# Input projections ahead of the memory rows' products, which move in between the first tile's attention heads

## The chip, the core and the metric

The kernel runs on one core of a Trainium2 chip. The metric is the device time of one execution in microseconds. TensorE (PE) multiplies, VectorE (DVE) and ScalarE (ACT) work on its results, GpSimd (POOL) issues the gathers of expert rows, and SyncE (SP) issues nearly all other transfers. Each engine takes its own instructions in order and waits on semaphores. PSUM holds the products, SBUF everything else.

## The reference, cut to what matters

```python
h   = rmsnorm(x, norm_mix)                      # x: 256 x 1024, float32
qkv_moba, qkv_fox, f = split(h @ w_in)          # w_in: 1024 x 3080, six blocks of 512 columns and 8 gates
o   = [rmsnorm(moba(...)), rmsnorm(fox(...))]   # 8 + 8 heads of 64, causal over 256 rows
x   = x + o @ w_out
mem_n = rmsnorm(mem, norm_mem)                  # mem: 256 x 1024
k, v = mem_n @ w_xk, mem_n @ w_xv               # needed only by the cross-attention
x   = x + softmax((rmsnorm(x) @ w_xq) @ k.T / 16) @ v @ w_xo      # 4 heads of 256
x   = x + peer_ffn(rmsnorm(x))                  # 16 of 16384 experts for each of 8 heads, rows gathered
out = rmsnorm(x, norm_final)
```

The sub-keys of `peer_ffn` (8 x 128 x 64, twice) are transposed once, in the kernel's step `skT`. The products with `w_in`, `w_xk` and `w_xv` don't depend on each other.

## The kernel before

**Tiles and order.** The 256 rows are two tiles of 128. One list, `main`, names the steps in the order in which every engine takes its part of them (lines 128 to 148); an engine skips steps in which it has no part. A step is (name, tile or block, half). There is no scheduler: the written order is the queue of each of PE, ACT and DVE, and SP has an order of its own (lines 390 to 434).

**Half blocks.** A weight block is 1024 x 512 (2 MB), a half block 256 of its columns. Float32 products are made out of three products of rounded parts: high x high, high x low, low x high. So a half block q needs a `split` first: ACT casts the high part into one of two buffers `WH_r[q % 2]` (line 527), DVE subtracts it in place to leave the low part (line 705), and PE then runs 48 matmuls of 128x128 by 128x256 (line 964). `projections(lo, hi)` puts `split` q+2 directly ahead of half block q in `main`. As `split` q+2 overwrites the high part that product q reads, ACT's cast waits until product q has ended, and what comes behind it in ACT's and DVE's queues waits too, the copy of product q out of PSUM first of all.

**The 20 half blocks.** Before: four of `w_xk` (steps `mK`), four of `w_xv` (`mV`), twelve of `w_in` (`winv`, whose result DVE copies, and `wina`, whose result ACT copies, in turn). Then come the 16 heads of tile 0 (8 MoBA, 8 FoX).

**A head.** `S` (PE line 1043, and for FoX 1047 too; DVE adds the mask and takes the minimum, line 750; ACT takes the exponential, line 555), `PT` (PE transposes the probabilities, line 1055; ACT copies, line 560), `O` (PE, line 1064). The heads are staggered: S two ahead, O one behind.

**PSUM banks.** There are two banks for results that DVE takes (`v_bank`: `memT`, `hT`, `winv`, `S`, `skT`, ...) and two for those that ACT takes (`a_bank`: `mK`, `mV`, `wina`, `PT`, ...). Job n of either sort waits until job n-2 of its sort has been copied out (`v_free`, `a_free`). PE is in order, so a transpose that waits for a bank holds up all products behind it.

**SP.** It loads the blocks into six slots in the order of use; a block waits for the last product of the block that had its slot. `bias_scratch` is written to memory and read back in eight pieces while SP waits for it. The sub-keys land in the buffer that held the high part of `h`, so their transfers wait for the last product with `h` (lines 418 to 424). Step `skT` (PE line 1009) stands behind `S` of the first two heads of tile 1.

## Time and profile before

| | us |
|---|---|
| median of three runs (1002.21 to 1005.22) | 1003.92 |
| the profiled execution, its own time | 1000.79 |
| its span in the trace | 999.0 |
| first product of a half block starts | 17.22 |
| last product with `w_in` ends, heads of tile 0 begin | 140.07 |
| last head product of tile 0 starts | 168.88 |
| first probabilities of tile 1 are transposed | 174.84 |
| first gather of expert rows is issued | 312.15 |

Of the whole span PE is busy for 85%, DVE 56%, ACT 42%. Up to 312 us the kernel is a chain of dense steps with hardly any gather; behind it 256 groups of expert rows are fetched at some 400 GB/s and worked off. The change touches only what lies before 174.84 us. The rows of the section below are read as follows: a row gives the start and the duration in us, the engine, the line in the kernel, the operation, `out<-in` with sizes, and in brackets how long the engine had been idle and for whom.

### The profile page before, as it was taken

To read this page: it belongs to the slowest core of one execution; us is meant where nothing else is said; L and a number is where in the kernel's file an instruction comes from. 1 tells how busy PE (TensorE), PEld (TensorE's weight loads), DVE (VectorE), ACT (ScalarE), POOL (GpSimd) and SP (SyncE) were. 2 spreads that over 40 slices of the span, in tenths; PEclk is the share of its full clock that TensorE was granted. 3 is DMA by queue.
4 is the path that set the end of the run, shared out by engine and by line. 5 is a ranking of instruction groups with operands and counts; after the bars stand their busy time and mean duration, and the time that the engine had idled before them with its cause. 6 is when DMAs were issued, how large, how long until landed. Compare 5 with 4: busy or idle time off the path is not lost.

```text
span 999.0 us, 9382 instructions
## 1 busy us (share of the span) xinstructions
PE 847.4 (85%) x3163; PEld 478.0 (48%) x3163; DVE 563.1 (56%) x1336; ACT 416.7 (42%) x1082; POOL 244.0 (24%) x267
## 2 busy tenths in 40 slices
PE   5999999999797988988879999887686877877876
PEld 4999986647745635533334355432232322322322
DVE  5544432112225757477686675758668587685743
ACT  5434434213302454356643543435354344343533
POOL 0000000000002332333333423333333333434330
PEclk9999995585998999999999999999999999999999
DMA  9869652000016998999999999999999999999995
GB/s 335 289 144 382 225 212 63 22 0 1 1 41 266 367 406 311 372 423 423 420 415 403 364 423 366 360 423 378 420 421 422 421 420 422 409 407 418 416 422 237
DMA packets 63299, 316.33 MB, mean 317 GB/s; under 512 B 7891, under 2 KB 10004, under 8 KB 30484
## 3 DMA queue, kind: packets, MB, share of 16 engines
q0 software_dynamic: 36864, 268.45, 65.9%
q1 hardware_dynamic: 26340, 47.28, 14.1%
q8 instruction: 25, 0.41, 0.2%
q14 instruction: 22, 0.18, 0.0%
q10 hardware_dynamic: 48, 0.01, 0.0%
HBM read 313.10 MB, written 2.62 MB: 316 GB/s over the span
## 4 chain that ended last, share of the span: by engine, by line
PE 48%; DMA 27%; DVE 15%; ACT 7%; issue 2%; POOL 0%; POOLq 0%; DVEq 0%; ACTq 0%
DMA qkvb<-in_expert_rows,expert_idx 20%; PE y L1152 10%; PE a_bank L964 8%; DMA spare<-in_expert_rows,expert_idx 7%; PE v_bank L1152 7%; PE a_bank L957 6%; PE v_bank L957 6%; DVE qkvb L890 5%; PE v_bank L964 4%; PE v_bank L1043 2%; PE y L1064 2%; DVE spare L890 2%; PE v_bank L1047 1%; ACT diag L617 1%; DVE key_idx L828 1%
## 5 line engine op out<-in xcount | busy, mean ns | idle before, releaser
L462 POOL DMA_INDIRECT qkvb<-in_expert_rows,expert_idx x172 | 162.1, 943 | 592.3 <-DVE expert_idx L866 309.7
L1152 PE MATMUL v_bank<-qkvb,diag 128*128 128x512 f32 x344 | 169.4, 627 | 48.7 <-ACT diag L617 48.7
L610 ACT ACTIVATE gelu<-dots 128x1 f32<-128x1 f32 x256 | 51.6, 202 | 347.6 <-DVE dots L890 347.2
L1152 PE MATMUL y<-qkvb,diag 128*128 128x512 f32 x344 | 166.1, 626 | 35.8 <-ACT diag L617 35.7
L890 DVE CUSTOM_DVE_ANT_0 qkvb<-h_psum,qkvb 128x1024 f32<-128x1024 f32 x86 | 104.2, 1223 | 75.0 <-DMA qkvb<-in_expert_rows,expert_idx 74.8
L890 DVE CUSTOM_DVE_ANT_0 qkvb<-a_bank,qkvb 128x1024 f32<-128x1024 f32 x86 | 104.2, 1223 | 69.6 <-DMA qkvb<-in_expert_rows,expert_idx 68.9
L1152 PEld LDWEIGHTS v_bank<-qkvb,diag 128*128 128x128 f32 x344 | 61.8, 193 | 155.7 <-ACT diag L617 103.2
L1152 PEld LDWEIGHTS y<-qkvb,diag 128*128 128x128 f32 x344 | 64.7, 197 | 126.3 <-issue 63.1
L462 POOL DMA_INDIRECT spare<-in_expert_rows,expert_idx x84 | 80.3, 956 | 142.0 <-PE y L1152 74.2
L617 ACT ACTIVATE diag<-ident,wgt 128x128 f32<-128x128 f32 x256 | 102.7, 401 | 8.3
L1152 PE MATMUL v_bank<-spare,diag 128*128 128x512 f32 x168 | 84.2, 634 | 22.3 <-ACT diag L617 22.3
L1152 PE MATMUL y<-spare,diag 128*128 128x512 f32 x168 | 77.9, 602 | 12.2 <-ACT diag L617 12.2
L614 ACT ACTIVATE wgt<-gelu,gates 128x1 f32<-128x1 f32 x256 | 75.4, 295 | 8.3
L705 DVE TENSOR_TENSOR weights_r<-weights,spare_r 128x2048 fp32r<-128x2048 f32 x20 | 45.7, 2291 | 54.3 <-ACT spare_r L527 54.3
L890 DVE CUSTOM_DVE_ANT_0 spare<-h_psum,spare 128x1024 f32<-128x1024 f32 x42 | 50.8, 1223 | 39.7 <-DMA spare<-in_expert_rows,expert_idx 39.6
L890 DVE CUSTOM_DVE_ANT_0 spare<-a_bank,spare 128x1024 f32<-128x1024 f32 x42 | 50.9, 1223 | 34.6 <-DMA spare<-in_expert_rows,expert_idx 34.4
L1152 PEld LDWEIGHTS v_bank<-spare,diag 128*128 128x128 f32 x168 | 30.5, 196 | 75.2 <-ACT diag L617 49.0
L527 ACT CAST spare_r<-weights 128x2048 fp32r<-128x2048 f32 x20 | 37.9, 1901 | 59.6 <-PE a_bank L964 43.1
L1152 PEld LDWEIGHTS y<-spare,diag 128*128 128x128 f32 x168 | 30.6, 191 | 52.8 <-issue 29.5
L957 PEld LDWEIGHTS a_bank<-x_and_h,weights 128*128 128x128 f32 x448 | 53.7, 201 | 3.6 <-issue 3.6
L957 PE MATMUL a_bank<-x_and_h,weights 128*128 128x128 f32 x448 | 53.9, 284 | 0.8 <-issue 0.8
L555 ACT ACTIVATE probs<-s_sb,neg_max 128x128 f32<-128x128 f32 (+1 forms) x32 | 14.5, 454 | 56.1 <-DVE neg_max L750 56.1
(194 smaller groups left out, 1163.1 us busy)
## 6 DMA issues: line engine op xcount, KB each, us to landing
weights<-in_w_in SPq DMA_DIRECT2D x6, 2048.0 KB, 18.5
weights<-in_w_xk SPq DMA_DIRECT2D x2, 2048.0 KB, 12.7
weights<-in_w_xv SPq DMA_DIRECT2D x2, 2048.0 KB, 15.5
weights<-in_w_out SPq DMA_DIRECT2D x2, 2048.0 KB, 18.3
weights<-in_w_xq SPq DMA_DIRECT2D x2, 2048.0 KB, 8.0
weights<-in_w_xo SPq DMA_DIRECT2D x2, 2048.0 KB, 8.2
weights<-in_w_peer_query SPq DMA_DIRECT2D x2, 2048.0 KB, 7.9
qkvb<-in_expert_rows,expert_idx POOLq DMA_INDIRECT x172
```

Source lines behind the costliest of these rows:

```text
L462: pool.indirect_dma_start(ROWS[n % NS], None, expert_rows, bass.IndirectOffsetOnAxis(ap=IDX[:, H % 3, k:k + 1], axis=0))\
L527: act.copy(WH_r[t % 2], half_block(t, W)).then_inc(high_ready, 1)
L610: nc.scalar.activation(gel[:, i:i + 1], dots[:, i:i + 1], ACT.Gelu).then_inc(gelu_done, 1)
L614: nc.scalar.activation(wgt[:, i:i + 1], gel[:, i:i + 1], ACT.Copy, scale=GATE[:, H % 3, k:k + 1])\
L617: nc.scalar.activation(diag[:, i, :], ident[:, :], ACT.Copy, scale=wgt[:, i:i + 1])\
L705: nc.vector.tensor_tensor(half_block(t, W_r), half_block(t, W), WH_r[t % 2].bitcast(f32), ALU.subtract).then_inc(low_ready, 1)
L890: nc.vector.tensor_tensor_reduce(out=ROWS[i][:, 0:D], in0=HP[n // SPT][:, :], in1=ROWS[i][:, 0:D], scale=1.0, scalar=0.0, op0=ALU.mult, op ...
L957: ins = nc.tensor.matmul(bank[:, lo:lo + n], lhs(k), rhs(k), start=(k == 0), stop=(k == chunks - 1))
L964: ins = nc.tensor.matmul(bank[:, lo:lo + n], a(k), b(k), start=(k == 0 and p == 0), stop=(k == KC - 1 and p == 2))
L1043: ins = nc.tensor.matmul(bank[:, 0:nk], Q[lo:lo + HD, t, c, :], K[lo:lo + HD, 0:t + 1, c, :], start=True, stop=i < NH)
L1064: ins = nc.tensor.matmul(y[:, i * HD:(i + 1) * HD], PT[:, n % 2, j * P:(j + 1) * P], V[:, j, i * HD:(i + 1) * HD], start=(j == 0), stop=(j ...
L1152: ins = nc.tensor.matmul(YP[t][:, b * BLK:(b + 1) * BLK], diag[:, i, :], ROWS[i][:, D + b * BLK:D + (b + 1) * BLK], start=False, stop=n % ...
```

## The change

The blocks' order becomes `w_in`, `w_xk`, `w_xv`. The rows of x are loaded, normed and transposed (`hT`) first. The memory rows are loaded behind the second block of `w_in`, and their steps (`root_m`, `scale_m`, `memT`, `m_parts`) stand between the third, fourth and fifth half products. The eight half products with the memory rows stand between tile 0's heads, one behind every second head. The memory rows' parts move out of Q, K into a slot of the weight buffer (slot 5), which later takes the second block of `w_xq`; so that block, and all that stands behind it in SP's queue (the first block of `w_peer_query`, the sub-keys, `w_xo`), waits for the last `mV` product.

```diff
@@ the block list and the slots @@
+MEM_SLOT = 5
...
-    for name, cols in (("w_xk", 2), ("w_xv", 2), ("w_in", 6), ("w_out", 2), ("w_xq", 2), ("w_xo", 2),
+    for name, cols in (("w_in", 6), ("w_xk", 2), ("w_xv", 2), ("w_out", 2), ("w_xq", 2), ("w_xo", 2),
                        ("w_peer_query", 2)):
         blocks += [(name, b) for b in range(cols)]
-    BN = {key: n for n, key in enumerate(blocks)}
+
+    SLOT = dict(zip(blocks, (0, 1, 2, 3, 4, 0, 1, 2, 3, 4, 0, 1, 2, MEM_SLOT, 3, 4, 0, 1)))
+    NTH = {key: [k for k in blocks if SLOT[k] == SLOT[key]].index(key) + 1 for key in blocks}
+    BEFORE = {key: [k for k in blocks if SLOT[k] == SLOT[key]][NTH[key] - 2] for key in blocks if NTH[key] > 1}
...
@@ the order of the steps @@
-    main = [("root_m", 0, 0), ("scale_m", 0, 0), ("root_m", 0, 1), ("scale_m", 0, 1), ("gains", 0, 0),
-            ("memT", 0, 0), ("memT", 0, 1), ("memT", 1, 0), ("memT", 1, 1), ("m_parts", 0, 0),
-            ("m_parts", 1, 0), ("split", 0, 0), ("split", 1, 0), ("bias", 0, 0), ("root_h", 0, 0), ("root_h", 1, 0),
-            ("scale_h", 0, 0), ("scale_h", 1, 0), half_job(0)]
-    main += [("hT", t, i) for t in range(T) for i in range(2)] + [("split", 2, 0)] + projections(1, 2)
-    main += projections(2, 3) + [("h_parts", 0, 0), ("h_parts", 1, 0), ("f_parts", 0, 0)]
-    main += projections(3, 8) + [("forget", 0, 0)]
-    main += projections(8, 10) + [("fsum", 0, 0)] + projections(10, len(halves))
-    main += heads(0, 0, 2 * NH) + [("o_out", 0, 0), ("o_out", 0, 1), ("o_root", 0, 0), ("o_root", 0, 1)]
+    def mem_tile(m):
+        return [("root_m", 0, m), ("scale_m", 0, m)], [("memT", m, 0), ("memT", m, 1), ("m_parts", m, 0)]
+
+    main = [("root_h", 0, 0), ("scale_h", 0, 0), ("root_h", 1, 0), ("scale_h", 1, 0), ("gains", 0, 0)]
+    main += [("hT", 0, 0), ("hT", 0, 1), ("split", 0, 0), ("h_parts", 0, 0), ("hT", 1, 0), ("hT", 1, 1),
+             ("h_parts", 1, 0), ("split", 1, 0), ("bias", 0, 0), ("f_parts", 0, 0)]
+    main += projections(0, 2) + mem_tile(0)[0] + projections(2, 3) + mem_tile(0)[1]
+    main += projections(3, 4) + mem_tile(1)[0] + projections(4, 5) + mem_tile(1)[1]
+    main += projections(5, 7) + [("forget", 0, 0)] + projections(7, 9) + [("fsum", 0, 0)] + projections(9, 12)
+    first = heads(0, 0, 2 * NH)
+    for h in range(2 * NH):
+        at = first.index(("O", 0, h))
+        main += first[:at]
+        first = first[at:]
+        if h % 2:
+            main += projections(12 + h // 2, 13 + h // 2)
+    main += first + [("o_out", 0, 0), ("o_out", 0, 1), ("o_root", 0, 0), ("o_root", 0, 1)]
...
@@ where the memory rows' copies lie @@
-        MH_r = QKVB_r[:, 0:2, :]
-        M_whole, ML_r = QKVB[:, 2:4, :], QKVB_r[:, 2:4, :]
+        MEMS, MEMS_r = [of[:, MEM_SLOT, :].rearrange("p (h m x) -> p h m x", h=2, m=2) for of in (W, W_r)]
+        MH_r = MEMS_r[:, 0, :, :]
+        M_whole, ML_r = MEMS[:, 1, :, :], MEMS_r[:, 1, :, :]
...
-        MEM = [Q[:, m, :, :].rearrange("p c x -> p (c x)") for m in range(2)]
-        MEMT = [K[:, m, :, :] for m in range(2)]
+        MEM = [MEMS[:, 0, m, :] for m in range(2)]
+        MEMT = [MEMS[:, 1, m, :].rearrange("p (c x) -> p c x", c=KC) for m in range(2)]
...
@@ SyncE: new queue @@
+            def load_block(name, b):
+                key = (name, b)
+                if key in BEFORE:
+                    sp.wait_ge(*used_up(*BEFORE[key]))
                 src = A[name][0].rearrange("(k p) c -> p k c", p=P)[:, :, b * BLK:(b + 1) * BLK]
+                sp.dma_start(W[:, SLOT[key], :].rearrange("p (k c) -> p k c", k=KC), src)\
+                    .then_inc(w_full[SLOT[key]], 16)
+
+            for t in range(T):
+                sp.dma_start(X[t], A["x"][0, t * P:(t + 1) * P, :]).then_inc(ld_x[t], 16)
             load_gain(sp, 1)
             load_gain(sp, 2)
+            load_block("w_in", 0)
             sp.wait_ge(rel_one, 1)
             sp.dma_start(relb[0:N_BUCKETS, :], A["rel_bias"]).then_inc(ld_rel, 16)
             sp.dma_start(onehot, A["bucket_rows"]).then_inc(ld_rel, 16)
             sp.dma_start(bf[:, :], A["b_forget"][0].rearrange("(h a) -> h a", a=1)).then_inc(ld_wf, 16)
             sp.dma_start(wf[:, :, :], A["w_in"][0].rearrange("(k p) c -> p k c", p=P)[:, :, 6 * BLK:6 * BLK + NH])\
                 .then_inc(ld_wf, 16)
+            load_block("w_in", 1)
+            for m in range(2):
+                sp.dma_start(MEM[m], A["mem"][0, m * P:(m + 1) * P, :]).then_inc(ld_mem[m], 16)
+            for b in range(2, 5):
+                load_block("w_in", b)
 
 
             sp.wait_ge(a_free, AN[("bias", 0, 0)] + 1)
             sp.dma_start(bias_scratch, brow.unsqueeze(1).broadcast_to([NH, P, FDIST])).then_inc(brow_out, 16)
             sp.wait_ge(brow_out, 16)
             for h in range(NH):
                 toeplitz = bass.AP(tensor=bias_scratch.tensor, offset=h * P * FDIST + P - 1,
                                    ap=[[FDIST - 1, P], [1, SEQ]])
                 sp.dma_start(B[:, h, :], toeplitz).then_inc(ld_bias, 16)
+            load_block("w_in", 5)
+            for name in ("w_xk", "w_xv", "w_out"):
+                for b in range(2):
+                    load_block(name, b)
+            load_block("w_xq", 0)
+
+
+            sp.wait_ge(a_full, AN[("mV", 1, 1)] + 1)
+            load_block("w_xq", 1)
+            sp.dma_start(wq_early, A["w_peer_query"][0].rearrange("(k p) c -> p k c", p=P)[:, :, 0:BLK])\
+                .then_inc(ld_early, 16)
+            for half, name in enumerate(("peer_subkeys_1", "peer_subkeys_2")):
+                sp.dma_start(sk_nat[:, :, half * HD:(half + 1) * HD], A[name][0].rearrange("h n d -> n h d"))\
+                    .then_inc(ld_sk, 16)
+            for b in range(2):
+                load_block("w_xo", b)
+            sp.wait_ge(v_full, VN[("skT", 0, 1)] + 1)
+            sp.dma_start(gffn[:, :], A["norm_ffn"][0:1, :].broadcast_to([P, D])).then_inc(ld_gffn, 16)
+            for b in range(2):
+                load_block("w_peer_query", b)
...
@@ ScalarE: the memory rows' square goes to hp, and root_h waits for nothing else @@
-                    root(key, MEM[i], V[:, i, :], D)
+                    root(key, MEM[i], hp[:, :], D)
                 elif name == "root_h":
                     act.wait_ge(ld_x[t], 16)
-                    act.wait_ge(sq_done, 2)
```

DVE's queue at the memory rows (`L662`/`L680` apply the gain to a transposed half of them, `L692`/`L710` take the low part, `L705`/`L723` is the subtraction of a split, `L736`/`L754` copies a `winv` product out of its bank). Before, at the start of the kernel:

```order
L678 COPY gain_cols<-v_bank 128x32
L662 TENSOR_TENSOR qkvb<-v_bank,gain_cols 128x512 x4
L692 TENSOR_TENSOR qkvb_r<-qkvb,qkvb_r 128x1024 x2
L705 TENSOR_TENSOR weights_r<-weights,spare_r 128x8x256 x2
L655 RECIPROCAL stat<-stat 128x1
L685 TENSOR_SCALAR qkvb<-x_and_h,stat 128x1024
```

Now, between the half products:

```order
L700 TENSOR_SCALAR weights<-weights,stat 128x1024
L723 TENSOR_TENSOR weights_r<-weights,spare_r 128x8x256
L754 TENSOR_SCALAR qkvb<-v_bank 128x2x2x128
L680 TENSOR_TENSOR weights<-v_bank,gain_cols 128x512 x2
L710 TENSOR_TENSOR weights_r<-weights,weights_r 128x1024
L723 TENSOR_TENSOR weights_r<-weights,spare_r 128x8x256
```

The gains of the memory rows moved from the kernel's start to behind a split and the copy of a product; PE has the eight transposes of a memory tile in one piece (`L969`) ahead of the fourth product, and again ahead of the sixth.

ACT's queue at the first heads (`L555`/`L573` is a head's exponential, `L560`/`L578` copies its transposed probabilities, `L527`/`L545` is the cast of a split, `L506`/`L525` copies a product with `w_xk`). Before:

```order
L555 ACT_TABLE_LOAD
L555 ACTIVATE probs,row_sum<-s_sb,neg_max 128x128 x2
L560 COPY probs_t<-a_bank 128x128
L555 ACTIVATE probs,row_sum<-s_sb,neg_max 128x128
L560 COPY probs_t<-a_bank 128x128
L555 ACTIVATE probs,row_sum<-s_sb,neg_max 128x128
L560 COPY probs_t<-a_bank 128x128
L555 ACTIVATE probs,row_sum<-s_sb,neg_max 128x128
L560 COPY probs_t<-a_bank 128x128
L555 ACTIVATE probs,row_sum<-s_sb,neg_max 128x128
L560 COPY probs_t<-a_bank 128x128
```

Now:

```order
L578 COPY probs_t<-a_bank 128x128
L573 ACTIVATE probs,row_sum<-s_sb,neg_max 128x128
L578 COPY probs_t<-a_bank 128x128
L573 ACTIVATE probs,row_sum<-s_sb,neg_max 128x128
L545 CAST spare_r<-weights 128x2048
L525 COPY mem_k<-a_bank 128x512
L578 COPY probs_t<-a_bank 128x128
L573 ACTIVATE probs,row_sum<-s_sb,neg_max 128x128
L578 COPY probs_t<-a_bank 128x128
L573 ACTIVATE probs,row_sum<-s_sb,neg_max 128x128
L545 CAST spare_r<-weights 128x2048
L525 COPY mem_k<-a_bank 128x512
```

A cast and the copy of a product came in behind every second head. The cast stands ahead of the product's copy and of the next head's copy and exponential.

SP's queue around the sub-keys. Before:

```order
L387 DMA weights<-in_w_in 128x8x512 x3
L387 DMA weights<-in_w_out 128x8x512 x2
L387 DMA weights<-in_w_xq 128x8x512 x2
L387 DMA weights<-in_w_xo 128x8x512 x2
L420 DMA spare<-in_w_peer_query 128x8x512
L423 DMA scaled_gffn<-in_peer_subkeys 128x8x64 x2
L426 DMA scaled_gffn<-in_norm_ffn 128x1024
```

Now:

```order
L400 DMA weights<-in_w_xv 128x8x512 x2
L400 DMA weights<-in_w_out 128x8x512 x2
L400 DMA weights<-in_w_xq 128x8x512 x2
L437 DMA spare<-in_w_peer_query 128x8x512
L440 DMA scaled_gffn<-in_peer_subkeys 128x8x64 x2
L400 DMA weights<-in_w_xo 128x8x512 x2
L445 DMA scaled_gffn<-in_norm_ffn 128x1024
```

The sub-keys stood behind both blocks of `w_xo` and behind the wait for the last product with `h`, which ended ahead of all heads; now they stand behind the second block of `w_xq`, and so behind the wait for the last `mV` product, which comes ahead of the last head's `O`. `w_xo` follows them.

## Rows read from the trace of the kernel before

**Rows 1.** the chain of waits, 0 to 420 us: start us, us, what (merged)

```profile
17.22 8.14 PE a_bank L964 x48
...
27.89 40.31 PE a_bank L964 x336
...
174.84 0.69 PE a_bank L1055 x2
```

**Rows 2.** by stretch: PE, PEld, DVE, ACT, POOL busy, PEclk, DMA share, GB/s

```profile
76.70:140.00 63.30, 63.30 (x528) 63.15 (x527) 27.92 (x19) 24.87 (x19) 0.00 (x0) 1.00 0.73 264
140.00:168.00 28.00, 26.01 (x89) 18.30 (x89) 4.68 (x32) 12.55 (x46) 0.00 (x0) 0.59 0.52 169
```

**Rows 3.** timeline of ACT, 60 to 100 us

```profile
68.30 1.91 ACT L527 CAST spare_r<-weights 128x2048 fp32r<-128x2048 f32 x1 [3.37 <-PE a_bank L964]
70.11 0.58 ACT L510 COPY mem_v<-a_bank 128x512 f32<-128x512 f32 x1
```

**Rows 4.** timeline of DVE, 60 to 100 us

```profile
78.72 2.29 DVE L705 TENSOR_TENSOR weights_r<-weights,spare_r 128x2048 fp32r<-128x2048 f32 x1 [5.04 <-ACT spare_r L527]
80.93 0.68 DVE L736 TENSOR_SCALAR qkvb<-v_bank 128x512 f32<-128x512 f32 x1
```

**Rows 5.** timeline of all engines, 0 to 28 us

```profile
7.98 0.69 DVE L662 TENSOR_TENSOR qkvb<-v_bank,gain_cols 128x512 f32<-128x512 f32 x1
...
11.78 2.42 DVE L692 TENSOR_TENSOR qkvb_r<-qkvb,qkvb_r 128x1024 fp32r<-128x1024 f32 x2
11.90 1.04 ACT L514 CAST qkvb_r<-qkvb 128x1024 fp32r<-128x1024 f32 x1 [0.92 <-DVE qkvb L662]
12.85 3.69 ACT L527 CAST spare_r<-weights 128x2048 fp32r<-128x2048 f32 x2
```

**Rows 6.** the weight tile's transfers issued 0 to 5 us: the first block

```profile
DMA to landing us min/median/max: 9.9/9.9/9.9
```

**Rows 7.** timeline of all engines, 138 to 178 us

```profile
140.09 0.58 ACT L542 COPY qkvb<-a_bank 128x512 f32<-128x512 f32 x1 [9.06 <-PE a_bank L964]
...
141.25 0.29 DVE L750 CUSTOM_DVE_ANT_0 s_sb<-v_bank,qkvb 128x128 f32<-128x128 f32 x1 [6.23 <-PE v_bank L1043]
...
143.21 0.33 PE L1055 MATMUL a_bank<-ident,probs 128*128 128x128 f32 x1
...
143.47 0.48 PE L1043 MATMUL v_bank<-qkvb 64*128 64x128 f32 x2
...
143.88 0.43 PE L1064 MATMUL y<-qkvb,probs_t 128*128 128x64 f32 x2
...
144.45 0.29 PEld L1043 LDWEIGHTS v_bank<-qkvb 64*128 64x128 f32 x2
...
168.88 1.25 PE L1064 MATMUL y<-qkvb,probs_t 128*128 128x64 f32 x4
...
171.90 1.94 PE L952 MATMUL v_bank<-ident,scaled_gffn 128*128 128x128 f32 x8 [0.61 <-DVE neg_max L750]
```

**Rows 8.** by stretch, as rows 2: the clock falls, PE busy and PE idle

```profile
144.00:145.00 1.00, 1.00 (x6) 0.74 (x7) 0.31 (x3) 0.94 (x6) 0.00 (x0) 1.00 1.05 410
145.00:146.00 1.00, 1.00 (x5) 0.78 (x5) 0.28 (x2) 0.66 (x3) 0.00 (x0) 0.50 1.04 401
...
318.00:320.00 2.00, 0.00 (x0) 0.00 (x0) 0.13 (x1) 0.56 (x1) 1.15 (x2) 0.77 1.03 430
```

**Rows 9.** SyncE's DMA issues, 0 to 310 us

```profile
69.66 3.67 SPq L415 DMA_DIRECT2D qkvb<-bias_scratch  x8
...
140.57 0.51 SPq L420 DMA_DIRECT2D spare<-in_w_peer_query  x1
141.12 9.13 SPq L423 DMA_DIRECT2D scaled_gffn<-in_peer_subkeys  x2
```

**Rows 10.** the two sub-key transfers, issued 141.12 and 144.5 us

```profile
DMA to landing us min/median/max: 11.4/12.7/14.0
```

**Rows 11.** by stretch, as rows 2: behind the sub-keys' landing

```profile
155.00:160.00 5.00, 5.00 (x16) 3.51 (x16) 0.60 (x4) 1.70 (x7) 0.00 (x0) 0.50 0.01 2
```

More of the change, by code:

```diff
@@ L280, in wslot @@
         def wslot(name, b):
-            return BN[(name, b)] % W_SLOTS
+            return SLOT[(name, b)]
         def wblk(name, b):
@@ L399, in _ @@
             sp.dma_start(onehot, A["bucket_rows"]).then_inc(ld_rel, 16)
-            load_block(1)
             sp.dma_start(bf[:, :], A["b_forget"][0].rearrange("(h a) -> h a", a=1)).then_inc(ld_wf, 16)
@@ L403, in _ @@
                 .then_inc(ld_wf, 16)
-            for n in range(2, W_SLOTS):
-                load_block(n)
+            load_block("w_in", 1)
[3 more added lines that the diff above has]
+                load_block("w_in", b)
             sp.wait_ge(a_free, AN[("bias", 0, 0)] + 1)
             sp.dma_start(bias_scratch, brow.unsqueeze(1).broadcast_to([NH, P, FDIST])).then_inc(brow_out, 16)
-            load_block(W_SLOTS)
             sp.wait_ge(brow_out, 16)
@@ L415, in _ @@
                 sp.dma_start(B[:, h, :], toeplitz).then_inc(ld_bias, 16)
-            for n in range(W_SLOTS + 1, len(blocks)):
-                if n == BN[("w_peer_query", 0)]:
-                    sp.wait_ge(a_full, AN[("wina", 5, 1)] + 1)
-                    sp.wait_ge(v_full, VN[("winv", 5, 0)] + 1)
-                    sp.dma_start(wq_early, A["w_peer_query"][0].rearrange("(k p) c -> p k c", p=P)[:, :, 0:BLK])\
-                        .then_inc(ld_early, 16)
-                    for half, name in enumerate(("peer_subkeys_1", "peer_subkeys_2")):
-                        sp.dma_start(sk_nat[:, :, half * HD:(half + 1) * HD], A[name][0].rearrange("h n d -> n h d"))\
-                            .then_inc(ld_sk, 16)
-                    sp.wait_ge(v_full, VN[("skT", 0, 1)] + 1)
-                    sp.dma_start(gffn[:, :], A["norm_ffn"][0:1, :].broadcast_to([P, D])).then_inc(ld_gffn, 16)
-                load_block(n)
+            load_block("w_in", 5)
[16 more added lines that the diff above has]
+                load_block("w_peer_query", b)
             sp.wait_ge(v_full, VN[("xo", 1, 0)] + 1)
@@ L520, in step @@
                     wname, b, half = halves[t]
-                    n = BN[(wname, b)]
-                    act.wait_ge(w_full[n % W_SLOTS], 16 * (n // W_SLOTS + 1))
+                    act.wait_ge(w_full[SLOT[(wname, b)]], 16 * NTH[(wname, b)])
                     if t >= 2:
@@ L942, in weights @@
             def weights(name, b):
-                n = BN[(name, b)]
-                pe.wait_ge(w_full[n % W_SLOTS], 16 * (n // W_SLOTS + 1))
+                pe.wait_ge(w_full[SLOT[(name, b)]], 16 * NTH[(name, b)])
                 return wblk(name, b)
```

11 lines of the change are left out of this document (removed).

## Prediction

> **What bounds the kernel now.** I read the chain of waits first, then the busy time by stretch, then the timelines of ACT and DVE beside a half product, last SyncE's issues and their landings. The chain shows where the change acts: the first half product runs from 17.22 for 8.14 us, and the next seven take 40.31 us without a gap, 5.76 us each (336 matmuls, 48 to a product) [rows 1]. From 76.70 to 140.00 PE is busy for 63.30 of 63.30 us at the full clock (granted share 1.00, 2.4 GHz); in the 28 us of tile 0's heads behind it PE is busy for 26.01 us, but at a mean share of 0.59 [rows 2]. So the reader is to see two stages, both bound by PE: a dense one, and one whose work is small and runs at 1.2 GHz. The heads take from 140.07 (ACT's copy of the last product starts at 140.09) to the last `O` at 168.88, 28.8 us; tile 1 goes on at 174.84 [rows 1, 7]. The idea worth testing is that the 46 us of memory products would cover the heads' waits and hold the clock up. What decides is whether PE can go from a head to a product and back without waiting for ACT and DVE.
>
> Beside a product these are not idle. Behind each product's end ACT casts (68.30 to 70.21) and only then copies the product out (70.11 for 0.58) [rows 3]: the bank is free 2.5 us after the product's end (which is 68.21, from rows 1: 27.89 + 40.31). DVE subtracts for 2.29 us and copies at 80.93 for 0.68 [rows 4]; that cast began at 76.79 by the same pattern, so a bank on DVE's side is free 4.9 us after the product's end. Before, all this lies under the next product of 5.76 us, since PE always has one with the other sort of bank.
>
> **The change part by part.** The number of half products (20), splits (20) and head steps is the same. I sum what comes ahead of 174.84.
>
> *Start.* Before, the first weight block landed at 2.37 + 9.9 = 12.3 us [rows 6], and x shared the DMA engines with it. Now x comes first and the block has the engines nearly to itself: some 1.3 us earlier by half a megabyte less at 410 GB/s [rows 8], so 11.0. Then in DVE's and ACT's order: cast 1.85, subtraction 2.29, low part of h 1.21 (half of 2.42), two gains of 0.69, and only behind those ACT's cast of the second tile's h 1.04 and its low part 1.21 [rows 5]. That is 9.0 us, a first product at 20.2 in place of 17.22: +3.0. If the block lands no earlier, +4.3; if the casts hid each other wholly as before, 0. I take 3.0. It starts at half clock as before, 8.14 us.
>
> *hT moved ahead.* The gap between the first and the second product, 25.36 (17.22 + 8.14) to 27.89, held the transposes of h [rows 1]. It goes: -2.5.
>
> *memT.* PE has eight transposes ahead of the fourth product and eight ahead of the sixth. The second four need the bank of the `winv` product that has just ended, and DVE copies that behind the split: 4.9 us, then four transposes of some 0.5 us (1.94 for eight at half clock [rows 7]). PE stands and the next product is behind: 5.5 us, twice, +11.0. Bounds: if DVE copied at once, little more than the transposes, 2.5 for both; at the high end nothing but the clock. The other additions on ACT (square 1.04, cast 1.04) and DVE (scale, low part 1.21) fit into the 5.76 us beside 2.5 and 3.0 us of split and copy, so 0; should ACT write the square to PSUM at twice the price it still fits.
>
> *The heads.* Three sorts of gap. (1) From the last `w_in` product to the first memory product: before, DVE took S of head 0 at 141.25; now the split's subtraction stands ahead of it and it starts at +4.3 (1.9 + 2.3, with a hand-over). From there to the end of head 4's S took 141.25 to 144.45 and 0.4 for the S [rows 7], 3.6 us: 7.9. (2) Behind six of the products a cast stands ahead of the product's copy on ACT. PE does O, PT, S, O in less than 1 us, then its PT wants the bank of that product: 2.5 us, then PT and S, 0.67 us (143.21 to 143.88 [rows 7]), with FoX's second matmul some 0.35 more. 3.2 once, 3.55 four times, 2.85 for the one without S. (3) Behind the seventh there is no cast: 0.8. Sum 7.9 + 3.2 + 14.2 + 2.85 + 0.8 = 28.95, against 28.8 before: 0. The heads no longer cost PE time at half clock; they cost waits of the same length. If the gaps were only the heads' own matmuls at full clock (S, O and PT from 143.47 to 144.45 [rows 7], 0.98 a head, with FoX's second matmul 1.33), 18.5 us: -10.3.
>
> *The clock.* It fell at 145, five us behind the last product, though PE was full of head work again, and elsewhere in the middle of 318 to 320, where PE was idle [rows 8]. The two memT gaps (5.5 us) and the 7.9 us one are like these. A product that begins at half clock cost 8.14 - 5.76 = 2.4 more [rows 1]: three times, +7.2, between 0 and 7.2. The seven short gaps: between 0 and 7 x 2.4 = 16.8; I take 0, since each holds only 1.8 us with PE idle, and keep 16.8 for the range.
>
> The Trainium skill ("TensorE: Matmul & The Clock Gate", HAM oscillation) describes the bad case: matmul bursts with waits between, each burst started cold. Rows 8 agree for long gaps; whether 3.3 us is one, no row shows. By the rule applied to every product the time is the first rival's.
>
> *Sub-keys.* Before, they were issued right behind the 140.07 end together with 4 MB of blocks, and the second landed at 144.5 + 11.4 = 155.9 (the first at 155.1) [rows 9, 10]; behind it the engines moved 2 GB/s [rows 11]. That lay under the heads, `skT` ran at 171.90. Now the same burst (w_xq's second block, w_peer_query's first, sub-keys) waits for the last mV product, behind which PE has one O, two S and then `skT`. Landing 15.8 us behind it, eight transposes 1.94, a hand-over: tile 1 goes on 17.9 us after the start of the last O, where it was 174.84 - 168.88 = 6.0. +11.9. Nothing covers it: DVE and ACT wait behind `skT` too. Bounds: 4.7 MB at the 430 GB/s of rows 8 are 10.9 us, so +7; with both transfers fully late (14.0 behind 144.5) +14.5.
> The Trainium skill ("DMA: Bandwidth & Descriptors", Queues, rings and completion order) says a ring's descriptors are consumed in order, so sub-keys can't overtake the blocks; by its 425 GB/s the estimate would be 11 us in place of 15.8.
>
> *Hidden.* The last w_in block now follows the write and read-back of the bias. If that read-back is issued at 69.66 as before [rows 9] and the block lands 10 to 19 us behind it, it is there by 92 at the latest; its split is due at about 93. 0, with a few us above. `w_xo` is loaded 20 us later but used far behind. The stages from 174.84 on keep their length, at half clock first as before, and the gathers start later by the sum.
>
> **Sum.** +3.0 - 2.5 + 11.0 + 0 + 7.2 + 11.9 = +30.6. The profiled execution took 1000.79 us, so 1031.4; it lies 3.1 below the median 1003.92, which gives 1034.5 for a median.
>
> **Rivals.**
> (A) Every product starts cold: the short gaps count as idle for the clock too. For: the heads kept it down with PE full. Against: between gaps stand 5.76 us of dense work. 1034.5 + 16.8 = 1051.
> (B) The sub-keys don't hold tile 1 up, or much less, and the clock stays up in the long gaps: 1034.5 - 11.9 = 1022.5; by the clock alone 1027. For: bytes alone need less than 15.8. Against: rows 10 and 11.
> (C) Not slower: the splits don't stand in the way. One mechanism, at every bank behind a product: the casts would run ahead, under the product before, so that the bank is free at the product's end. Then memT costs 2.5 in place of 11.0, the heads -10.3, the start's +3.0 goes and the clock holds (-7.2): 1034.5 - 29.0 = 1005.5, inside 0.3%; with the sub-keys by bytes alone (-4.9) 1000.6. It decides from the point where a product's copy follows it within 1 us. Against it: rows 3, where the cast comes first, and the written order keeps it so.
> (D) It doesn't do what it says, e.g. the last w_in block late: some 5 to 10 us more, in the range.
>
> **How the numbers follow.** Forecast 0.72, with its own range 1024 to 1045; (A) 0.12; (B) 0.10; (C) 0.06, a third of it faster. Range 1021 to 1048: it leaves out (C) and most of (A). A measurement of this kernel tells 0.3%, 3 us, from no change. Faster 0.02, within 0.04, slower 0.94.
>
> **What would show it.** First product at 20 to 21.5 us; PE idle over 4 us ahead of the second four memT transposes, twice; last w_in product ending near 110; six gaps of 3.2 to 3.6 us between memory products, in which PT waits for ACT's copy; the last mV product ending near 187; `skT` waiting for DMA to near 203, PT of tile 1 near 205. Wrong would be: a first product before 18, memory products back to back, `skT` without a wait, or a stage behind 205 that is shorter than before's.

## The result and the profile after

| | before | after |
|---|---|---|
| median of the runs, us | 1003.07 (4 runs) | 1051.66 (1047.82 to 1055.28, 4 runs) |
| ratio, 95% interval | | 1.0483 (1.0439 to 1.0527) |
| the profiled execution, its own time | 1000.79 | 1051.51 |
| its span | 999.0 | 1049.7 |
| first half product starts, us from the span's start | 17.22 | 21.30 |
| last `w_in` product ends | 140.07 | 112.08 |
| last memory product ends | 68.21 | 204.69 |
| tile 1 goes on (first transposed probabilities) | 174.84 | 222.31 |
| first gather of expert rows | 312.15 | 358.79 |

The changed kernel is 4.8% slower: 48.6 us by the medians, 50.7 by the two profiled executions. 47.5 us of it stand at 222.31, where tile 1 goes on; up to the first gather nothing is added (46.6), and behind it 4.1 (690.9 against 686.8 us), of which more below. One execution of all that are told of below, of the kernel of experiment 9, took 1083.7 us at a mean granted clock of 0.73, where its others had 0.93 to 0.94; it is left out.

The page's second part of the changed kernel shows PE's busy tenths and its granted clock in 40 slices of 26 us:

```profile
PE   3889789769989798898788989987778878778786
...
PEclk7889877858599999899999999999999999999999
```

Before had six nines and then two slices at 5 (the heads, from 150 us on). Now the second to the eighth slice read 8, 8, 9, 8, 7, 7, 8. The first slice says nothing on the change: the trace of before shows a share of 1.00 there, although its first product took 8.14 us with 0.41 us for a matmul in place of 0.28. There the duration tells the clock, not the share. The chain of waits of the changed kernel (start us, us, what), which answers to rows 1:

```profile
21.30 8.64 PE v_bank L981 x48
...
43.48 2.29 DVE weights_r L723
45.77 0.61 DVE qkvb L754
...
46.52 1.09 PE v_bank L969 x4
47.61 7.36 PE a_bank L981 x48
...
66.88 7.90 PE a_bank L981 x48
...
112.16 1.91 ACT spare_r L545
...
114.15 2.15 issue
...
121.05 8.28 PE a_bank L981 x48
...
132.65 7.45 PE a_bank L981 x48
...
144.14 8.62 PE a_bank L981 x48
...
198.66 6.03 PE a_bank L981 x48
...
208.99 11.30 DMA scaled_gffn<-in_peer_subkeys
...
222.31 0.43 PE a_bank L1072 x2
```

Each step stands where the prediction put it. The first product starts at 21.30. Ahead of the fourth product DVE subtracts, copies the third, PE transposes, and the product (47.61) takes 7.36 us. Behind the last `w_in` product (112.08) come ACT's cast and DVE's subtraction (the row of 2.15, for which the profile names no releaser), and the first memory product starts at 121.05. Then the products themselves: 8.28, 7.45, 8.62 and so on, 6.03 for the last. Seven of the eight are far from the 5.76 of [rows 1]; the prediction had that for the first alone.

The timeline of one gap between two memory products in the changed kernel (start us, us, engine, instruction; what lies between one product's end and the next one's start I call a gap, whether PE is busy in it or not), which answers to rows 3 and 7:

```profile
129.40 1.90 ACT L545 CAST spare_r<-weights 128x2048 fp32r<-128x2048 f32 x1 [7.49 <-PE a_bank L981]
...
129.94 0.43 PE L1081 MATMUL y<-qkvb,probs_t 128*128 128x64 f32 x2
131.21 0.58 ACT L525 COPY mem_k<-a_bank 128x512 f32<-128x512 f32 x1
...
131.93 0.30 PE L1072 MATMUL a_bank<-ident,probs 128*128 128x128 f32 x1 [1.56 <-ACT mem_k L525]
...
132.58 0.51 PE L981 MATMUL a_bank<-weights_r,spare_r 128*128 128x256 f32 x2
```

The product's last matmul ended at 129.3. PE did O, PT, S and O up to 130.4, then stood for 1.56 us until ACT's copy of the product, behind the cast, had freed the bank; PT at 131.93, next product at 132.58. This is the predicted gap of 3.2 us, to a tenth (3.25 by this timeline, 3.32 by the chain). What the clock made of it, by stretch (columns as rows 2, the third number from the end is the granted share):

```profile
44.00:45.00 1.00, 0.00 (x0) 0.00 (x0) 1.00 (x1) 0.00 (x0) 0.00 (x0) 0.67 0.45 49
...
132.00:133.00 1.00, 1.00 (x6) 0.76 (x7) 1.00 (x1) 0.00 (x0) 0.00 (x0) 1.00 0.00 0
133.00:134.00 1.00, 1.00 (x7) 1.00 (x6) 1.00 (x5) 0.13 (x1) 0.00 (x0) 0.55 0.09 16
```

In the wait for the memory rows' bank the share falls at 44.3, 2.9 us behind the product's end, with PE idle all that time. In the heads it falls at 133.1, though PE had stood for only 1.56 us and was in the next product already. SyncE's issues of the changed kernel, answering to rows 9:

```profile
163.94 41.13 SPq L400 DMA_DIRECT2D weights<-in_w_xq  x2
205.12 0.58 SPq L437 DMA_DIRECT2D spare<-in_w_peer_query  x1
205.75 8.45 SPq L440 DMA_DIRECT2D scaled_gffn<-in_peer_subkeys  x2
```

The block of `w_xq` waited to 204.7, and the sub-keys are behind it; the landing in the chain (208.99 + 11.30 = 220.3) is 15.6 us behind the last product's end, against 15.8 in [rows 9, 10]. The blocks issued ahead of them landed ahead of them, `w_xq`'s at 212.4 and `w_peer_query`'s at 218.0.

### The profile page after: what moved, and what is told of

Read it like the earlier page. It is cut to its first block, busy times and chain, and to the rows that moved or that the text cites. A ratio compares the mean times of both kernels' runs of the same rounds, so it can differ in the third digit from the quotient of the medians.

```text
span 1049.7 us, 9379 instructions
## 1 busy us (share of the span) xinstructions
PE 860.5 (82%) x3163; PEld 490.4 (47%) x3163; DVE 562.1 (54%) x1336; ACT 415.2 (40%) x1082; POOL 243.3 (23%) x267
## 4 chain that ended last, share of the span: by engine, by line
PE 45%; DMA 29%; DVE 14%; ACT 7%; issue 3%; SPq 1%; POOL 0%; POOLq 0%; ACTq 0%; DVEq 0%
DMA qkvb<-in_expert_rows,expert_idx 19%; PE a_bank L981 9%; PE y L1169 9%; DMA spare<-in_expert_rows,expert_idx 9%; PE v_bank L1169 6%; PE a_bank L974 6%; PE v_bank L974 5%; DVE qkvb L908 4%; PE v_bank L981 4%; DVE spare L908 2%; PE v_bank L1060 2%; PE y L1081 1%; ACT diag L635 1%; DVE key_idx L846 1%; DMA scaled_gffn<-in_peer_subkeys 1%
## 5 line engine op out<-in xcount | busy, mean ns | idle before, releaser
L1169 PE MATMUL v_bank<-qkvb,diag 128*128 128x512 f32 x344 | 173.0, 638 | 47.3 <-ACT diag L635 47.3
L723 DVE TENSOR_TENSOR weights_r<-weights,spare_r 128x2048 fp32r<-128x2048 f32 x20 | 45.8, 2292 | 107.4 <-ACT spare_r L545 107.4
L1169 PE MATMUL v_bank<-spare,diag 128*128 128x512 f32 x168 | 82.3, 621 | 22.4 <-ACT diag L635 22.4
L545 ACT CAST spare_r<-weights 128x2048 fp32r<-128x2048 f32 x20 | 38.0, 1900 | 92.0 <-PE a_bank L981 64.8
L974 PEld LDWEIGHTS a_bank<-x_and_h,weights 128*128 128x128 f32 x448 | 53.3, 199 | 3.7 <-issue 3.7
L981 PE MATMUL a_bank<-weights_r 128*128 128x256 f32 x128 | 42.4, 331 | 0.0
```

The source lines that it names most:

```text
L545: act.copy(WH_r[t % 2], half_block(t, W)).then_inc(high_ready, 1)
L723: nc.vector.tensor_tensor(half_block(t, W_r), half_block(t, W), WH_r[t % 2].bitcast(f32), ALU.subtract).then_inc(low_ready, 1)
L974: ins = nc.tensor.matmul(bank[:, lo:lo + n], lhs(k), rhs(k), start=(k == 0), stop=(k == chunks - 1))
L981: ins = nc.tensor.matmul(bank[:, lo:lo + n], a(k), b(k), start=(k == 0 and p == 0), stop=(k == KC - 1 and p == 2))
L1169: ins = nc.tensor.matmul(YP[t][:, b * BLK:(b + 1) * BLK], diag[:, i, :], ROWS[i][:, D + b * BLK:D + (b + 1) * BLK], start=False, stop=n % ...
```

## The experiments

All ratios are against the kernel before, run on the same chip as the kernels of its group; its medians in these groups were 1001.9 to 1002.6 us. "The changed kernel" is 1051.7, from the group of the result, where before had 1003.1: a difference from it in us is good to a us or two, and where it matters the point at which tile 1 goes on (222.31 in the changed kernel) is given from the traces.

**1. Memory products in one piece, ahead of the heads.**

```diff
+    main += projections(12, len(halves))
     first = heads(0, 0, 2 * NH)
...
-        if h % 2:
-            main += projections(12 + h // 2, 13 + h // 2)
```

> Edit: the changed kernel, but the eight memory products stand in one piece behind the input products and ahead of tile 0's heads (no interleaving); block order, start, memory rows' steps and SyncE's queue stay as changed. Theory (the interleaving costs): the stretch from the last input product's end to the last head's O took 92.6 us in the changed kernel, where 8 x 5.76 + 28.8 = 74.9 would do without interleaving; and the sub-keys, issued behind the last memory product, again land under the heads (-11.6): 1051.7 - 17.7 - 11.6 = 1022. Rival (the loss is in the start and the memory rows' transposes, or behind the heads, and interleaving is neutral): no more than the 11.6 us of the sub-keys, 1040. The clock in the memory products should be 1.00 throughout and each 5.76 us.

1020.1 us (before in this group 1001.9), ratio 1.0186 (1.0152 to 1.0220). From 111 to 158 us, by stretch:

```profile
111.00:158.00 47.00, 46.71 (x390) 46.38 (x388) 16.31 (x10) 17.96 (x17) 0.00 (x0) 1.00 0.39 135
```

Clock 1.00, PE busy for 46.71 of 47 us. Interleaving, with the late sub-keys that it brings, cost 31.5 us. The rest of the loss, 18 us, lies in what this kernel shares with the changed one, the start and the memory rows' transposes. The rival is out.

**2. The gaps filled with dense work.**

```diff
                 elif name == "PT":
                     n = SN[(t, i)]
+                    if t == 0 and i in (4, 6, 8, 10, 12, 14):
+                        for k in range(14):
+                            nc.tensor.matmul(hp[:, 0:HC], h_high(k % KC)[:, 0, :], h_high(k % KC),
+                                             start=True, stop=True)
                     pe.wait_ge(p_ready, n + 1)
```

> Edit: the changed kernel with 14 more dense matmuls (128x128 by 128x256, of the normed rows with themselves, into an unused bank, results not read) put into six of the gaps between memory products, right ahead of the PT that waits for ACT's copy. PE has more to do and nothing waits less. Theory (it is the clock: gaps of 3.2 to 4.0 us let it fall, and the products behind them run at 1.2 GHz for a part): seven products behind such gaps took 7.45, 8.62, 7.43, 8.66, 7.44, 7.32 and 6.03 us; six of them go to 5.76 with a granted clock of 1.00, 12 us less: 1040, although PE executes 84 matmuls (10 us) more. Rival (the products are slow since ACT and DVE work beside them, or since the gap itself costs): no gain, 1052, or up to 10 us slower if the added matmuls don't fit into the wait.

1038.8 us, ratio 1.0372 (1.0333 to 1.0411): 12.9 us less than the changed kernel, with more to do. The chain of this run at the first gap:

```profile
129.24 0.37 PE y L1085 x2
129.60 1.71 PE h_psum L1071 x14
131.32 0.15 PE a_bank L1076
131.47 0.41 PE v_bank L1060 x2
131.88 5.95 PE a_bank L981 x48
```

The 14 matmuls (1.71 us) fill what was a wait, the gap is still 3.3 us long, and the product behind it takes 5.95 us, not 7.45; so do the next five (5.94 or 5.95, the sixth 5.77). By stretch, the whole of the heads in this run and in the changed kernel:

```profile
111.00:194.00 83.00, 78.17 (x571) 72.42 (x569) 20.85 (x42) 29.02 (x65) 0.00 (x0) 0.94 0.22 77
...
112.20:204.70 92.50, 80.12 (x480) 73.97 (x480) 20.61 (x41) 28.55 (x64) 0.00 (x0) 0.80 0.20 69
```

From 126 us on, behind the first product, the share of this run is 1.00 up to 194; what is missing to 1.00 in its row lies ahead of that. The gaps behind products got no shorter (all seven together 23.5 us in place of 22.4), and the neighbours on ACT and DVE are the same; only PE's own activity in the gaps differs. The six products fell from 46.9 to 35.5 us, by 11.4. So it is the clock, and not the waits or a contention, that lengthened the products. This is the run that settles the missed term.

**3. Splits one product later between the heads.**

```diff
-    main += projections(5, 7) + [("forget", 0, 0)] + projections(7, 9) + [("fsum", 0, 0)] + projections(9, 12)
+    main += projections(5, 7) + [("forget", 0, 0)] + projections(7, 9) + [("fsum", 0, 0)] + projections(9, 11) + [half_job(11)]
...
-            main += projections(12 + h // 2, 13 + h // 2)
+            q = 12 + h // 2
+            main += ([("split", q + 1, 0)] if q + 1 < len(halves) else []) + [half_job(q)]
```

> Edit: the changed kernel, but between the heads split q+1 stands ahead of product q (its buffer has been free since product q-1 ended), in place of split q+2, which had to wait for product q itself; the split ahead of the last input product goes too. The same work, interleaved in the same places. Theory (gaps come from the cast standing ahead of the product's copy on ACT, and the clock falls in them): the copy follows the product's end at once, gaps shrink from 3.2 to 4.0 us to 1.3 to 2 us, products go to 5.76 us but the first (some 8), head 0 starts 3 us earlier: the stretch goes from 92.6 to about 65 us, 1051.7 - 28 = 1024. Rival (the heads' own chain from S over DVE and ACT to PT and O sets the gaps): gaps stay over 3 us, 1045 to 1052.

1022.7 us, ratio 1.0211 (1.0168 to 1.0254), 29 us less than the changed kernel. Its chain:

```profile
116.43 8.34 PE a_bank L982 x48
124.78 0.17 PE y L1082 x2
...
125.84 0.12 PE a_bank L1073
...
126.37 5.95 PE a_bank L982 x48
```

The gap is 1.6 us (124.78 to 126.37), all of it matmuls, and the products take 5.95. From the last `w_in` product's end (111.07) to the last memory product's (179.44) it is 68.4 us, in place of 92.6. Of these 24.2 us, 3.6 are the first wait, shorter since the split ahead of the last input product is gone, and 20.6 the gaps and products behind it. Only the first product (8.34) still starts cold, behind a wait of 5.4 us for the first exponentials. This is the same interleaving, place for place, without the cast in ACT's way: the gaps came from the queue's order, and the heads' chain doesn't set them.

**4. Sub-keys issued early.** In SyncE's queue the two transfers go behind the first `w_out` block, with a wait for the last products with `h`.

```diff
-            for name in ("w_xk", "w_xv", "w_out"):
-                for b in range(2):
-                    load_block(name, b)
+            for name, b in (("w_xk", 0), ("w_xk", 1), ("w_xv", 0), ("w_xv", 1), ("w_out", 0)):
+                load_block(name, b)
+            sp.wait_ge(v_full, VN[("winv", 5, 0)] + 1)
+            for half, name in enumerate(("peer_subkeys_1", "peer_subkeys_2")):
+                sp.dma_start(sk_nat[:, :, half * HD:(half + 1) * HD], A[name][0].rearrange("h n d -> n h d"))\
+                    .then_inc(ld_sk, 16)
+            load_block("w_out", 1)
...
-            for half, name in enumerate(("peer_subkeys_1", "peer_subkeys_2")):
-                sp.dma_start(sk_nat[:, :, half * HD:(half + 1) * HD], A[name][0].rearrange("h n d -> n h d"))\
-                    .then_inc(ld_sk, 16)
```

> Edit: the changed kernel, but the two sub-key transfers are issued behind the first block of w_out (right after the last input product), in place of behind the second block of w_xq and the wait for the last memory product. Theory (tile 1 waited 11.6 us for the sub-keys alone): the wait of skT goes and tile 1's first transposed probabilities follow the last O by about 6 us, not 17.6: 1051.7 - 11.6 = 1040. Rival (something else is as late, the table load and the exponentials, or the freed transfers collide with others): less than half of that, over 1046.

1034.5 us, ratio 1.0329 (1.0280 to 1.0378), 17 us less; expected were 11.6. The chain of this run behind the last product (202.16):

```profile
203.41 1.28 ACT L503
...
205.96 1.28 ACT L574
...
207.90 0.44 PE a_bank L1073 x2
```

Now the two table loads and the exponentials of ACT end last, as before the change, and tile 1 goes on 5.7 us behind the last product (17.6 in the changed kernel): 11.9 us, the predicted term. The last product itself ended 2.5 us earlier than in the changed kernel with nothing changed on PE, ACT or DVE. The trace has most of it at the start: the first block landed 9.2 us behind its issue in place of 10.0, the first product started at 20.55 in place of 21.30 and took 7.78 in place of 8.64 us, and the products behind the two waits for the memory rows took 0.6 us less together. Such a shift is no effect of the edit. The rest of the 17 is in the difference of two medians with some us between their runs.

**5. Copy and memory transposes ahead of the split.**

```diff
-    main += projections(0, 2) + mem_tile(0)[0] + projections(2, 3) + mem_tile(0)[1]
-    main += projections(3, 4) + mem_tile(1)[0] + projections(4, 5) + mem_tile(1)[1]
+    def swapped(q, m):
+        return mem_tile(m)[0] + [half_job(q)] + mem_tile(m)[1][:2] + [("split", q + 2, 0)] + mem_tile(m)[1][2:]
+    main += projections(0, 2) + swapped(2, 0) + projections(3, 4) + swapped(4, 1)
```

> Edit: the changed kernel, but the third and the fifth input product's copy and the memory rows' transposes stand ahead of the next split in the list, no longer behind it. Theory (PE stood for 6.1 us twice, since DVE's copy of the product stood behind the split's subtraction, and the clock fell in it): PE's two gaps go from 6.1 to about 1.5 us each (copy 0.7, transposes 0.5), the products behind them from 7.36 and 7.90 to 5.76: -9.2 - 3.7 = -13, 1039. Rival (the split comes later now and the product after next waits for its low part): -9 + a wait of 1 to 4 us twice, 1043 to 1050.

1036.9 us, ratio 1.0330 (1.0290 to 1.0369), 14.8 us less. The chain at the first tile of memory rows:

```profile
35.32 5.78 PE v_bank L983 x48
...
41.12 0.70 DVE qkvb L756
41.82 0.14 issue
41.96 0.63 PE v_bank L971 x4
42.59 5.75 PE a_bank L983 x48
```

The gap is 1.5 us (41.10 to 42.59) in place of 6.1, and the product behind it takes 5.75 in place of 7.36. The later split costs nothing.

**6. The start's order.** The four `hT` steps and both `h_parts` ahead of `split` 0.

```diff
-    main += [("hT", 0, 0), ("hT", 0, 1), ("split", 0, 0), ("h_parts", 0, 0), ("hT", 1, 0), ("hT", 1, 1),
-             ("h_parts", 1, 0), ("split", 1, 0), ("bias", 0, 0), ("f_parts", 0, 0)]
+    main += [("hT", 0, 0), ("hT", 0, 1), ("hT", 1, 0), ("hT", 1, 1), ("h_parts", 0, 0),
+             ("h_parts", 1, 0), ("split", 0, 0), ("split", 1, 0), ("bias", 0, 0), ("f_parts", 0, 0)]
```

> Edit: the changed kernel, but the transposes of both x tiles and both casts of h stand ahead of the first split. Theory (the first product started 4.1 us later since the second tile's gains and low part stood behind the first split): it starts at 17.3 in place of 21.3: -4, 1047.7. Rival (the first weight block's landing at 12.3 us sets it and all else is beside it): no change, 1051.

1046.5 us, ratio 1.0424 (1.0378 to 1.0471), 5.2 us less; the first product starts at 17.22 in its chain, to the hundredth as before. The block landed at 11.9 here (12.3 in the kernel before and in the changed one), and the chain no longer passes through it, but through the rows of x, their transposes and casts, and then the split. In the changed kernel 9.0 us of work stood between the landing and the first product.

**7. All four mended.**

> Edit: the changed kernel with all four mended: splits one product later between the heads, sub-keys issued behind the first w_out block, copies and memory transposes ahead of the split, and all four hT transposes and both casts of h ahead of the first split (first product at 17.3 as before, -4). Theory (the terms are of one chain and add up): 1051.7 - 29 - 17 - 13 - 4 = 989 in place of about 1003 of before: faster by 1.4%. Rival (they overlap: what one gives back another takes, as each wait hides the next): 1000 to 1010, no better than before.

996.6 us (8 runs), ratio 0.9929 (0.9899 to 0.9959): faster than before, but by 0.7% in place of 1.4%. Tile 1 goes on at 169.04, 5.8 us ahead of before and 53.3 ahead of the changed kernel. The four single runs, each read at that same point, had given 5.2, 13.9, 14.4 and 25.2, together 58.7. A small new wait is in the chain:

```profile
68.57 10.21 DMA weights<-in_w_in
...
78.80 1.91 ACT spare_r L549
...
83.17 5.99 PE v_bank L985 x48
```

The last `w_in` block, behind the write and the read-back of the bias, now is due before it lands: the late block that the prediction had under (D), here worth 1 us (PE stands for 1.00 us ahead of this product, which starts at 83.17; in the kernel of 8, where the same block came sooner, it starts at 82.28). Of the 5.4 us between 58.7 and 53.3 that is 1.0. Another 3.5 were no effects of the edits: the shift of 2.5 in experiment 4, and 1.0 in experiment 3, whose last `w_in` product also ended earlier (111.07 in place of 112.08) though nothing that PE waited for ahead of it was changed. The last 1 us is less than what the first product alone differs between the profiled executions (7.1 to 8.6 us). So the four terms add up but for about a us. The expected 989 took 29 and 17 from medians, which had given more than the traces.

**8. First memory product behind the S of heads 0 and 1.** The four mended, and besides each product two heads earlier.

```diff
-        main += first[:at]
+        if h == 0:
+            main += first[:2] + [("split", 13, 0), half_job(12)]
+            main += first[2:at]
+        else:
+            main += first[:at]
...
+        if h % 2 and h < 15:
+            q = 13 + h // 2
+            main += ([("split", q + 1, 0)] if q + 1 < len(halves) else []) + [half_job(q)]
```

> Edit: as the kernel with four mended, but the first memory product stands right behind the S of heads 0 and 1, ahead of their PT, and the others two heads earlier each. Theory (PE waits 5.4 us behind the last input product for the first heads' exponential, and the clock falls in it; the product behind took 8.34 in place of 5.76): the product covers the table load and the exponentials, the clock holds: -3 to -4 of the gap and -2.6, less 1 to 2 us for two heads without a product at the end: 5 us below the kernel with four mended, 984. Rival (the end of the heads then runs with its own waits and lets the clock fall there instead): within 2 us of it.

990.0 us (5 runs), ratio 0.9870 (0.9841 to 0.9899), 6.6 us below the kernel of 7; 5 were expected, from the 989 that the kernel of 7 had missed. Its chain at the first heads:

```profile
94.70 0.49 PE v_bank L1068 x4
95.20 5.96 PE a_bank L989 x48
...
101.91 0.30 PE a_bank L1080
102.20 0.42 PE v_bank L1068 x2
102.62 0.36 PE y L1089 x2
...
103.51 5.95 PE a_bank L989 x48
```

The first memory product follows the two S without a wait and takes 5.96, the gap behind it is 2.4 us, and the clock stays at 1.00 over 94 to 158 us. Tile 1 goes on at 163.34, 11.5 us ahead of before. The end of the heads did not become the new cold place: behind the last product (157.43) the share stayed at 1.00 up to 163.7.

**9. The same without interleaving.** The start, the copies and the memory transposes mended, products in one piece.

> Edit: the memory products in one piece ahead of the heads, as in the run with products first, and besides the mended start and the mended memory transposes (sub-keys are hidden there anyway). Theory (an interleaving without waits is worth what the heads cost at half clock): products first took 1020.1; less 13 to 14 and 4 to 5 it comes to 1001 to 1003, as before, and 11 to 13 us above the kernel with a product behind the first two S, which differs from it by the interleaving and the later splits alone. Rival (the gain of the mended kernels comes from the order of the blocks and not from interleaving): 990 to 995.

1004.1 us (median of 11 runs), ratio 1.0035 (1.0012 to 1.0057): with the order of the blocks alone the kernel is where it was, or 0.1 to 0.6% slower. Its tile 1 goes on at 175.81 (174.84 before), behind ACT's exponentials and not behind the sub-keys, so their place in the queue doesn't count here. The kernel of 8 goes on 12.5 us earlier and is 14.1 us faster by the medians. That is the interleaving's, when nothing waits in it.

**10. The last input block's load ahead of the wait for the bias write**, in the kernel of 8.

> Edit: the kernel with a product behind the first two S, and the last input block's load issued ahead of the wait for the bias write, in place of behind the read-back. Theory (its landing at some 79 us holds the eleventh product by 1 us or less in this kernel): the wait goes, 0 to 1 us faster, not to be told from 990.0. Rival (the block's transfer slows the bias write, whose read-back the first head needs, or the memory transfers): slower by 2 us and more.

991.6 us (6 runs), ratio 0.9903 (0.9871 to 0.9935): not to be told from 990.0. The expectation holds. The wait for the bias write was no longer for the block beside it (22.79 to 65.07), so the rival is out too.

## Why the prediction was wrong

The direction, the place and the order of all waits were right; what the prediction had wrong is what the clock does in the short gaps. The time was outside the range by 3.7 us at the top: 1034.5 forecast (1021 to 1048), 1051.7 measured. By the predicted steps, against the chain after:

| step | predicted | measured |
|---|---|---|
| start | +3.0 | +4.1 |
| first product, slower still | 0 | +0.5 |
| hT moved ahead | -2.5 | -2.5 |
| memT, two waits | +11.0 | +12.3 (6.1 and 6.1) |
| heads, gaps alone | 0 | +2.6 (31.4 against 28.8) |
| clock behind the three long gaps | +7.2 | +6.3 (1.6, 2.1, 2.5) |
| products behind the seven short gaps | 0 | +12.6 (11.4 of it the clock) |
| sub-keys | +11.9 | +11.7 |
| sum | +30.6 | +47.5 |

**Start.** The estimate that the first block would land 1.3 us earlier failed: it landed at 12.3 again, and in the runs, whose queues all begin as the changed kernel's does, at 11.6 to 13.0. The work behind the landing was 9.0 us as summed, and the upper bound that was given, +4.3, was near (its 20.2 has 0.2 us that no term names). The +0.5 of the first product is within the spread of the profiled executions, 7.1 to 8.6 us.

**Clock, the step that failed.** "The seven short gaps: between 0 and 7 x 2.4 = 16.8; I take 0, since each holds only 1.8 us with PE idle." Measured are 12.6 us: the products took 7.45, 8.62, 7.43, 8.66, 7.44, 7.32 and 6.03 us. For the first six the clock fell each time, inside the product or just ahead of it, though PE had stood for only 1.1 to 1.6 us, less than the 1.8 of the prediction. Run 2 prices it at 11.4 us, by filling the idle part, and run 3 removes it by shortening the gap. The other 1.2 us were no clock: a product behind head work takes 5.95 at the full share too (runs 2 and 3), and the last one 6.03.

The mistake was to take 1.8 us of idle time for harmless with no row that said so. [Rows 8] were read as "PE was full of head work again", and that holds for the 2.5 us ahead of 145 alone. The trace of before has two waits between the last product's end (140.07) and the fall:

```profile
140.73 0.49 PE L1043 MATMUL v_bank<-qkvb 64*128 64x128 f32 x4 [0.68 <-ACT qkvb L542]
142.53 0.33 PE L1055 MATMUL a_bank<-ident,probs 128*128 128x128 f32 x1 [1.31 <-ACT probs L555]
```

That is 2.0 us idle out of 4.9, much like the 1.1 to 1.6 out of 2.9 to 4.0 of the new gaps: a warning that stood in the record. What the same trace shows of head work alone is that it didn't bring the clock back. From 145 to 168.88 PE was busy without a pause, and the share stayed at 0.50. Whether it is the idle time or the whole time without a product that lets the clock fall, no run separates: the gaps at which it held (run 2, 3.3 to 4.2 us, filled; run 3, 1.6 to 2.4 us; run 8, 1.6 to 2.4 us) are shorter in both respects, counted without the filling. Nor is there one delay: the fall came 2.9 us behind the product's end in the first wait for the memory rows, 3.8 in the gap shown above, and 6.3 at the end of run 8's heads.

The +2.6 in the gaps are in part the same cause. 1.1 of it is the first gap (9.0 in place of 7.9), whose last 4.8 us ran at a share of 0.50. 0.6 is in two FoX gaps of 4.0 us, where the share fell ahead of the product and the second S took 0.72 in place of 0.41 us. The rest is 0.1 to 0.2 us a gap at the full share.

Rival (A), with its 0.12, was nearly what happened; its time was 1051, and that it came out at the measured one is partly luck, since 4.2 of the 16.8 didn't come and the gaps and the stage behind made up for it. Nor did the range do what the prediction says of it: the 16.8 was to be kept "for the range", and 1034.5 + 16.8 lies 3.3 us above its top.

The Trainium skill ("TensorE: Matmul & The Clock Gate", HAM oscillation) describes bursts of matmuls with waits between, each burst started cold. The prediction weighed it and found that no row spoke on a gap of 3.3 us. Now rows do, and the trace agrees in part: the clock fell for each of six products, but PE stood for only 1.1 to 1.6 us in a gap, and four of the six products still began at the full share.

**memT, heads, sub-keys.** Right to 1.3, 2.6 and 0.3 us. The queue rule (a cast behind the product that waits for it, ahead of that product's copy) gave the gap of 3.2 us as 3.25. The late sub-keys are shown by run 4, the memT waits by run 5. The sub-keys' landing came from the rows of before (15.8 us, measured 15.6); their bytes alone would have given 10.9.

**Behind tile 1's start** the forecast was 0, and the profiled executions have +3.2, all of it behind the first gather. In every variant the stage from there to the end took 687 to 692 us against 686.8 in the profile of before, in the ones that are faster than before too. The execution profiled of before lies 2.3 us below its median, so part of the 4.1 is the choice of the execution. A cause of the rest is not shown.

**The idea of the change was sound**, which the prediction gave little room: rival (C), banks free at a product's end, was held to be out of reach with the written order, and it was; with another order it is worth 12.5 us against before (run 8).

## What to carry to other kernels

A dense block put between latency-bound steps hides them only if no queue makes its neighbours wait for it: look at what stands behind the instruction that waits for the block's end (here a cast for the block after next, ahead of the copy that frees the bank), and give it a place where its wait is over already. Don't take a short wait of TensorE as free for its clock: look at each gap between dense stretches, with its light matmuls, and at the duration of the stretch behind it. Here gaps of 2.9 to 4.0 us with 1.1 to 1.6 us idle cost 1.5 to 2.7 us each, and gaps of 1.6 to 2.4 us none. And when a buffer gets a new late user, follow the transfer queue behind it to the first load that the critical path needs.

## What the runs showed that I had not expected

The clock fell while the next product was already running: the share dropped at 133.1, 0.5 us into the product that began at 132.58, and was back to 1.00 by 137. So a fall costs also where the gap is over. The two sorts of product, 7.4 and 8.6 us in turn, differ by where it came: some 0.5 us into the product (7.3 to 7.5), or already in a gap of 4.0 us, 0.7 to 0.8 us ahead of the product (8.6 and 8.7).

A product at the full clock takes 5.76 us behind another product and 5.95 behind S (runs 2, 3 and 8).

The write of the bias (1.5 MB from 8 partitions) took 41.5 to 43.2 us from its issue to the read-back in all twelve kernels, with or without the sixth block beside it: 28.12 to 69.66 before, 22.37 to 64.61 in the changed kernel, 22.41 to 64.83 in the kernel of 7.
